# The first 65 microseconds of a two-block kernel: load order, a constant tile for TensorE, and when the first modulation is turned

## The chip, the cores and the metric

The kernel runs on one core of one Trainium2 chip. The metric is the device time of one execution in microseconds (us), as the median of several runs. All data are float32. The five engines run their own instruction streams and meet at semaphores: TensorE (PE, with its weight loads shown as PEld), VectorE (DVE), ScalarE (ACT), GpSimd (POOL) and SyncE (SP), which here issues all the DMAs. A float32 matmul of the program appears in the trace as two records.

## The reference, cut to what matters

The program computes a first block (an mLSTM mixer beside a Hyena mixer, then a mixture of 16 experts) and then two layers of a second block. Only the start of the first block is touched by the change:

```python
mod = (c @ w_ada[l] + b_ada[l])[:, None, :]
sh1, sc1, gt1, sh2, sc2, gt2 = jnp.split(mod, 6, axis=-1)
h = rms_norm(x, g_mix[l]) * (1 + sc1) + sh1
p = h @ w_in[l] + b_in[l]                       # w_in is 1024 x 3600
q, k, v, o, gates, hx = jnp.split(p, split_pts, axis=-1)
filt = hyena_filters(seq_len, ...)              # see below
y_h = hyena_mixer(hx, conv_hy_w[l], conv_hy_b[l], filt, hy_bias[l], hyena_norm_g[l])

def hyena_filters(L, w1, b1, w2, b2, w3, freq, deltas):
    hid = jnp.sin(fr * (z @ w1 + b1))           # z: 256 x 33 constant features
    hid = jnp.sin(fr * (hid @ w2 + b2))         # 256 x 64
    h = hid @ w3                                # 256 x 2048
    window = jnp.exp(-t * jnp.abs(deltas)) + HYENA_WINDOW_SHIFT
    return (h * window).reshape(L, HYENA_ORDER, HYENA_DIRS, HYENA_WIDTH)
```

x is 256 tokens by 1024 features. The filters are needed as spectra (two orders, each a real and an imaginary part, from a DFT written as matmuls), and the Hyena mixer splits hx into x1, x2 and z.

## The kernel before

Every engine's order is written out by hand; there is no scheduler. What goes before what on an engine is the order of the calls.

**Weights** come as a stream of 2 MB tiles (`stream`) into a ring of four such slots. SP issues them in order, and issues tile n when the slot that it needs is released by the matmuls that read it (`release`, `release_with`). The stream before starts ada0 to ada4, z, x1, q, ada5, x2, ... An "ada" tile is a quarter of the rows of a third of w_ada; four of them (ada0 to ada3) make the first 2048 columns of the modulation, in which the shift sh1 and the scale sc1 of h lie. A z, x1, q, ... tile is 512 columns of w_in.

**Modulation.** `ada()` takes the next step on each engine. On TensorE it multiplies one tile (`ada_rows`, L1255, 16 records). All of a third's tiles are summed in PSUM bank 7, the only bank for this. After the third's last tile ACT copies the row out of the bank. The step after that first multiplies the next tile (which waits for bank 7 to be free) and then turns the row into columns (`ada_turn`, L1272), which DVE adds to its bias (`turned`, L1800). From them DVE makes the scale A1 (L1869), and DVE (L1872) and ACT (last four row tiles) make h, which the projections wait for (`h_ready`, `ht_scaled`).

**Filters.** Two small matmuls, hid1 (L1287, 33 rows) and hid2 (L1291, 64 rows), each followed by some DVE arithmetic and a sine on ACT; then eight matmuls with 64 rows and 512 columns (L1299). ACT makes the decay windows from `dlt` (the decay rates `hy_deltas`, broadcast to all partitions) and a column of `minus_t`, which lies in the table `tab`. DVE multiplies windows and filters (L1841) and adds and subtracts the halves (L1843, L1844). `spectrum(o)` (L1310, eight records) is the DFT of order o; ACT and DVE bring it out of PSUM.

**Norm.** GpSimd squares x, TensorE sums the squares with a matrix of ones (`sums`, L1281), ACT and DVE make 1/rms (L1848) and DVE scales x with it (L1850).

**TensorE's order before** is hid1, hid2, ada0, filters, sums, ada1, spectrum(0), ada2, ada3, ada4 and turn, spectrum(1), project z, project x1. After that follow gates, q and the rest of the block (L1236 is the line of all those projections). The instances of `ada` behind this stretch keep their places in the change.

**SP's order before** is the small filter inputs, the parameters, ada0, the tables, `dlt`, x, ada1 to ada3, four small inputs (b_v, b_gates, w_gates, w_router), then the stream.

## Time and profile before

| | before |
|---|---|
| time, median of 3 runs | 2253.46 us (2251.59 to 2253.8) |
| span of the profiled execution | 2255.7 us |
| TensorE busy | 2007.8 us, 89% |
| VectorE, ScalarE, GpSimd busy | 582.6, 417.7, 194.1 us |
| DMA | 664.24 MB, mean 294 GB/s |

The profiled execution took 2.2 us more than the median. The table of 40 slices (56.4 us each) shows how the limits change: in the first slice TensorE has 7 tenths while the DMA engines are nearly full; in slices 2 and 3 TensorE is full and the DMA engines are half idle; from slice 6 to slice 25 (some 282 to 1410 us) the DMA engines are full at about 420 GB/s, which is the expert part; after that it is TensorE that is full.

### The profile page before, as it was taken

The page shows a single profiled execution, that of the slowest core. Times are in us where ns is not written, and L with a number is a line of the kernel's source. Part 1 is how long each engine was busy: PE and PEld are TensorE (multiplying, and loading weights), DVE is VectorE, ACT ScalarE, POOL GpSimd, SP SyncE. Part 2 cuts the span into 40 slices and gives each one's busy share as a digit, 9 for nine tenths or more (in the row PEclk, how much of TensorE's full clock was granted, in tenths as well). Part 3 has the DMA queues.
Part 4 walks back from the last instruction along what each step waited for, and adds up shares of the span by engine and source line. Part 5 has one row for each costly group of instructions (what it writes and reads, how often), then busy time and mean ns, then how long its engine had stood idle before and what let it go on. Part 6 is the DMA issues. An engine that isn't in the chain of part 4 may idle for free.

```text
span 2255.7 us, 32640 instructions
## 1 busy us (share of the span) xinstructions
PE 2007.8 (89%) x14140; PEld 1405.5 (62%) x14140; DVE 582.6 (26%) x1187; ACT 417.7 (19%) x766; POOL 194.1 (9%) x183
## 2 busy tenths in 40 slices
PE   7999889887888888987888877999999999999997
PEld 3866666542445545653565543756888877588886
DVE  5267220104421100000001201454432034630001
ACT  2122121202310100000000311435200033630001
POOL 0530000002000000000000000135000003600000
PEclk9999989898899999998999999999999999999999
DMA  9548899999999999999999999530487842144450
GB/s 364 207 171 332 325 421 424 400 426 425 409 388 426 426 426 420 421 417 423 420 419 426 426 379 414 141 135 23 165 298 226 192 148 82 34 148 151 126 154 19
DMA packets 181286, 664.24 MB, mean 294 GB/s; under 512 B 17335, under 2 KB 121304, under 8 KB 142552
## 3 DMA queue, kind: packets, MB, share of 16 engines
q1 hardware_dynamic: 181144, 662.15, 75.2%
q8 instruction: 112, 1.84, 0.3%
q14 instruction: 30, 0.25, 0.0%
HBM read 661.08 MB, written 1.05 MB: 294 GB/s over the span
## 4 chain that ended last, share of the span: by engine, by line
PE 47%; DMA 21%; ACT 4%; DVE 3%; issue 1%; POOL 0%; SPq 0%; ACTq 0%; DVEq 0%; POOLq 0%
PE ps L1148 19%; PE ps L650 9%; DMA ring<-in_context_weights 7%; DMA ring<-in_w_gate 6%; DMA ring<-in_w_down_slots 5%; PE ps L1531 4%; DMA ring<-in_w_up 3%; PE ps L1557 2%; PE ps L984 2%; PE ps L1157 2%; PE ps L951 2%; ACT arena L2434 1%; PE ps L846 1%; PE ps L676 1%; PE ps L1060 1%
## 5 line engine op out<-in xcount | busy, mean ns | idle before, releaser
L1148 PE MATMUL ps<-arena,ring 128*128 128x256 f32 x1984 | 429.9, 379 | 1.0 <-DVEq L389 0.9
L1148 PEld LDWEIGHTS ps<-arena,ring 128*128 128x128 f32 x1984 | 376.5, 190 | 54.2 <-issue 1.7
L1531 PE MATMUL ps<-ring,arena 128*32 128x256 f32 x4032 | 259.7, 404 | 87.7 <-DMA ring<-in_w_up 45.2
L650 PE MATMUL ps<-arena,ring 128*128 128x256 f32 (+2 forms) x1372 | 310.5, 386 | 6.7 <-DMA ring<-in_context_weights 6.6
L650 PEld LDWEIGHTS ps<-arena,ring 128*128 128x128 f32 (+2 forms) x1372 | 249.7, 188 | 73.8 <-DMA ring<-in_context_weights 24.3
L1531 PEld LDWEIGHTS ps<-ring,arena 128*32 128x32 f32 x4032 | 126.1, 114 | 205.3 <-DMA ring<-in_w_up 59.1
L2141 ACT ACTIVATE arena<-ps 128x512 f32<-128x512 f32 (+3 forms) x143 | 76.7, 536 | 740.3 <-PE ps L650 332.2
L1557 PE MATMUL ps<-ring,arena 128*32 128x512 f32 x1024 | 141.4, 682 | 58.8 <-DMA ring<-in_w_down_slots 51.9
L1557 PEld LDWEIGHTS ps<-ring,arena 128*32 128x32 f32 x1024 | 30.5, 119 | 155.9 <-DMA ring<-in_w_down_slots 85.2
L1236 PE MATMUL ps<-arena,ring 128*128 128x256 f32 x512 | 112.0, 380 | 1.4 <-DMA ring<-in_w_out 1.4
L2946 POOL TENSOR_TENSOR XC<-XC,arena 128x256 f32<-128x256 f32 x32 | 23.4, 730 | 992.5 <-ACT XC L2235 972.2
L1236 PEld LDWEIGHTS ps<-arena,ring 128*128 128x128 f32 x512 | 96.9, 190 | 18.1 <-issue 5.2
L2956 POOL TENSOR_SCALAR arena<-arena 128x512 f32<-128x512 f32 x48 | 78.7, 1639 | 82.4 <-DVE arena L2851 79.1
L650 PE MATMUL ps<-ring,arena 128*128 128x256 f32 (+3 forms) x312 | 85.7, 426 | 0.0
L951 PE MATMUL ps<-arena,ring 128*128 128x256 f32 x352 | 78.6, 381 | 3.9 <-DMA ring<-in_context_weights 3.9
L2605 DVE SCALAR_TENSOR_TENSOR XC<-ps,arena,XC 128x256 f32<-128x256 f32 x48 | 23.2, 484 | 225.8 <-PE ps L1148 144.3
L1773 ACT ACTIVATE arena<-ps 128x256 f32<-128x256 f32 x32 | 12.3, 384 | 357.7 <-PE ps L1531 357.6
L951 PEld LDWEIGHTS ps<-arena,ring 128*128 128x128 f32 x352 | 66.2, 190 | 18.5 <-DMA ring<-in_context_weights 8.3
L650 PEld LDWEIGHTS ps<-ring,arena 128*128 128x128 f32 x312 | 54.5, 190 | 26.9 <-issue 17.1
L2110 DVE TENSOR_TENSOR arena<-arena,ps 128x256 f32<-128x256 f32 x32 | 13.5, 421 | 214.9 <-ACT arena L1773 213.9
L2900 DVE TENSOR_TENSOR arena<-arena,ps 128x512 f32<-128x512 f32 x20 | 13.8, 688 | 212.3 <-PE ps L1148 212.3
L1255 PE MATMUL ps<-ring,arena 128*32 128x512 f32 x448 | 56.9, 636 | 10.7 <-DMA ring<-in_w_ada 9.0
(359 smaller groups left out, 1940.9 us busy)
## 6 DMA issues: line engine op xcount, KB each, us to landing
ring<-in_w_up SPq DMA_DIRECT2D x64, 2048.0 KB, 13.2
ring<-in_w_down_slots SPq DMA_DIRECT2D x64, 2048.0 KB, 14.4
ring<-in_w_gate SPq DMA_DIRECT2D x62, 2048.0 KB, 14.0
ring<-in_w_ada SPq DMA_DIRECT2D x36, 2048.0 KB, 9.8
ring<-in_w_ffn_in SPq DMA_DIRECT2D x44, 1024.0 KB, 7.7
ring<-in_context_weights SPq DMA_DIRECT2D x35, 1024.0 KB, 14.5
ring<-in_w_ffn_out SPq DMA_DIRECT2D x16, 1408.0 KB, 7.0
ring<-in_w_in SPq DMA_DIRECT2D x9, 2048.0 KB, 8.0
```

Source lines behind the costliest of these rows:

```text
L650: m = mm(o, a, x, start=(k == 0 and r == 0), stop=(k == kt - 1 and last))
L951: m = mm(b[i][:, T * x:T * x + T], w[:, k % 2, c:c + P], HID[:, k, :], start=(k == 0 and x == 0), stop=(k == 21 and x == 1))
L984: m = mm(b[:, 0:RAW], w[:, k, c:c + P], raw[:, k, :], start=(k == 0), stop=(k == KD - 1))
L1148: m = mm(b, w[:, k, c:c + P], src[:, k, :], start=(k == 0), stop=(k == kt - 1))
L1157: m = mm(b[:, 0:T], held["w"][:, k, c:c + P], oT[X][:, k, :], start=(k == 0), stop=(k == KD - 1))
L1236: m = mm(b[:, T * i:T * i + T], w[:, k, P * (j + i):P * (j + i) + P], src(k), start=(k == 0), stop=(k == ktiles - 1))
L1255: m = mm(row_bank[0][32 * g:32 * g + 32, :], cpad[:, 2 * h + k, :], w[:, k, W * g:W * g + W], start=(h == 0 and k == 0), stop=(h == 3 and ...
L1531: m = mm(b[u][32 * c:32 * c + 32, T * x:T * x + T], xs[:, 2 * h + k, CAP * e:CAP * e + CAP], w[:, k, at_:at_ + T], start=(h == 0 and k == ...
L1557: m = mm(b[a][64 * n + 32 * j:64 * n + 32 * j + 32, :], hdT[:, 2 * a + j, ch, :], w[:, j, at_:at_ + W], start=(i == 0 and odd == 0), stop= ...
L2141: step(a(dst, src, f, **kw), frees=name if frees else None)
L2946: step(nc.gpsimd.tensor_tensor(hat[st][n % 2][:, x, :], ex[st][n % 2][:, x, :], glqk[:, x, :], ALU.mult), lev_ready if x else None)
L2956: step(nc.gpsimd.tensor_scalar(Pr[n % 8], Pr[n % 8], sm[:, n % 8:n % 8 + 1], None, ALU.mult), pn_ready[X])
```

## The change

1. **Loads.** `dlt` and x go ahead of ada0, and the tables behind it. `minus_t` moves from the tables into the parameters, so that the windows need only `dlt` and the parameters. `dlt` has a semaphore of its own; GpSimd's convolutions wait for the parameters in place of the tables.
2. **Stream.** z takes the place of ada4 in the stream, and ada4 comes behind z. SP issues z ahead of the four small inputs.
3. **Constant tile.** DVE sets a tile of 640 columns to 1.0 as its first instruction. TensorE multiplies it one time ahead of hid1, two times behind it and four times behind hid2 (128x128 by 512 columns, into bank 7, never read).
4. **TensorE's order.** The filters are cut in two halves of four matmuls, with ada0 between them.
5. **The first turn** comes as a step of its own right behind ada3. h follows at once on DVE and ACT. ada4 and spectrum(1) come behind project z, and DVE's and ACT's work on spectrum(0) comes behind h.
6. A semaphore that nothing waited for (`gqa_normed_ctx`) is gone.

The core of the diff (the wait for `c_ready` of the first ada tile becomes 2, because the constant tile uses its first count):

```diff
-                    if i and i % 4 == 0:
+                    if i == 4:
+                        turn(tiles[3][0], 0)
+                        continue
+                    i -= i > 4
...
+                    if i > 4 and i % 4 == 0:
                         turn(tiles[i - 1][0], tiles[i - 1][1] // 4)
...
+            def warming(count):
+
+                for _ in range(count):
+                    mm(ps[ADA_BANKS[0]][:], warm[:, 0:P], warm[:, P:P + W], start=True, stop=True)
+
+            pe.wait_ge(c_ready, 1)
+            warming(1)
             pe.wait_ge(s_hid, 48)
...
+            step(v.memset(warm, 1.0), c_ready)
...
-            spectrum(0)
             ada(5)
             step(stt(out=A1, in0=mod[:, 8:16], scalar=1.0, in1=pc("g_mix", 0, 8), op0=ALU.add, op1=ALU.mult))
...
             tell(h_ready)
+            spectrum(0)
+            ada()
             spectrum(1)
```

TensorE's instructions from the start, before (L1255 is one ada tile for every 8, L1299 filters, L1281 sums, L1310 a spectrum, L1272 the turn, L1236 the projections):

```order
L1287 MATMUL ps<-arena 64x256
L1291 MATMUL ps<-arena 64x256
L1255 MATMUL ps<-ring,arena 32x512 x8
L1299 MATMUL ps<-arena 128x512 x8
L1281 MATMUL ps<-arena,tab 128x256 x8
L1255 MATMUL ps<-ring,arena 32x512 x8
L1310 MATMUL ps<-arena,tab 128x512 x4
L1255 MATMUL ps<-ring,arena 32x512 x24
L1272 MATMUL ps<-tab,arena 128x4 x4
L1310 MATMUL ps<-arena,tab 128x512 x4
L1236 MATMUL ps<-arena,ring 128x256 x64
```

The same stretch of the changed kernel, where L1294 is the constant tile, L1261 an ada tile, L1313 the filters, L1287 the sums, L1321 a spectrum, L1278 the turn and L1242 a projection:

```order
L1305 MATMUL ps<-arena 64x256
L1294 MATMUL ps<-arena 128x512 x4
L1313 MATMUL ps<-arena 128x512 x4
L1261 MATMUL ps<-ring,arena 32x512 x8
L1313 MATMUL ps<-arena 128x512 x4
L1287 MATMUL ps<-arena,tab 128x256 x8
L1261 MATMUL ps<-ring,arena 32x512 x8
L1321 MATMUL ps<-arena,tab 128x512 x4
L1261 MATMUL ps<-ring,arena 32x512 x16
L1278 MATMUL ps<-tab,arena 128x4 x4
L1242 MATMUL ps<-arena,ring 128x256 x32
L1261 MATMUL ps<-ring,arena 32x512 x8
```

One ada tile (ada4) and one spectrum, which stood beside the turn, now stand behind the first 32 matmuls of the projections (z).

SP's DMAs behind the parameters, before:

```order
L3001 DMA ring<-in_w_ada 128x2x2048
L3004 DMA tab<-in_tables 128x2878
L3005 DMA arena<-in_hy_deltas 128x2048
L3006 DMA XC<-in_xT 128x8x256
L3001 DMA ring<-in_w_ada 128x2x2048 x3
L3009 DMA arena<-in_b_v 128x512
```

And in the changed kernel:

```order
L3028 DMA arena<-in_hy_deltas 128x2048
L3029 DMA XC<-in_xT 128x8x256
L3026 DMA ring<-in_w_ada 128x2x2048
L3031 DMA tab<-in_tables 128x2876
L3026 DMA ring<-in_w_ada 128x2x2048 x3
L3026 DMA ring<-in_w_in 128x8x512
L3034 DMA arena<-in_b_v 128x512
```

The 2 MB of ada0 went from ahead of three loads to between them, and z (the w_in tile) to ahead of the small inputs.

## Rows read from the trace of the kernel before

**Rows 1.** The page: the span in 40 slices of 56.4 us.

```profile
PE   7999889887888888987888877999999999999997
...
DMA  9548899999999999999999999530487842144450
```

**Rows 2.** Timeline of PE, 0 to 60 us: start, us, engine, line, operation, count [idle before].

```profile
...
8.53 1.08 PE L1291 MATMUL ps<-arena 64*64 64x256 f32 x2 [3.91 <-ACT arena L1604]
14.14 3.64 PE L1255 MATMUL ps<-ring,arena 128*32 128x512 f32 x16 [4.53 <-DMA ring<-in_w_ada]
17.71 14.02 PE L1299 MATMUL ps<-arena 64*128 64x512 f32 x16
31.66 6.09 PE L1281 MATMUL ps<-arena,tab 128*128 128x256 f32 x16
...
43.16 3.64 PE L1255 MATMUL ps<-ring,arena 128*32 128x512 f32 x32
47.66 1.93 PE L1255 MATMUL ps<-ring,arena 128*32 128x512 f32 x16 [0.87 <-ACT arena L1604]
49.52 1.06 PE L1272 MATMUL ps<-tab,arena 128*128 128x4 f32 x8
50.44 3.68 PE L1310 MATMUL ps<-arena,tab 128*128 128x512 f32 x8
53.95 6.42 PE L1236 MATMUL ps<-arena,ring 128*128 128x256 f32 x29
```

**Rows 3.** DMA issues: KB, us from issue to landing (first row ada3 alone).

```profile
ring<-in_w_ada SPq DMA_DIRECT2D x1, 2048.0 KB, 20.5
...
tab<-in_tables SPq DMA_DIRECT2D x1, 1439.0 KB, 12.9
arena<-in_hy_deltas SPq DMA_DIRECT2D x1, 1024.0 KB, 15.0
XC<-in_xT SPq DMA_DIRECT2D x1, 1024.0 KB, 17.4
...
par<-in_params SPq DMA_DIRECT2D x1, 193.0 KB, 4.7
```

**Rows 4.** Timeline of SP, 0 to 60 us (the last row ends with ada3's issue).

```profile
3.43 0.59 SPq L2990 DMA_DIRECT2D par<-in_params  x1
...
4.56 0.46 SPq L3004 DMA_DIRECT2D tab<-in_tables  x1
5.06 0.43 SPq L3005 DMA_DIRECT2D arena<-in_hy_deltas  x1
5.54 0.43 SPq L3006 DMA_DIRECT2D XC<-in_xT  x1
...
17.38 0.57 SPq L3001 DMA_DIRECT2D ring<-in_w_ada  x1
```

**Rows 5.** Timeline of ACT and DVE around the filters and around h.

```profile
12.97 0.42 ACT L1604 ACTIVATE arena<-arena 64x256 f32<-64x256 f32 x1 [4.58 <-DVE arena L1829]
...
22.28 0.69 DVE L1841 SCALAR_TENSOR_TENSOR arena<-arena,ps 128x512 f32<-128x512 f32 x1 [9.41 <-ACT arena L1604]
...
36.80 0.69 DVE L1844 TENSOR_TENSOR arena<-arena 128x512 f32<-128x512 f32 x1
...
50.68 0.17 DVE L1800 TENSOR_TENSOR arena<-ps,par 128x16 f32<-128x16 f32 x1 [2.60 <-PE ps L1272]
...
51.15 2.50 ACT L1604 ACTIVATE arena<-arena 128x256 f32<-128x256 f32 x4 [3.63 <-DVEq L389]
```

**Rows 6.** Busy us and granted clock by stretch: stretch, length, PE (x) to POOL (x), PEclk.

```profile
227.00:230.00 3.00, 0.32 (x4) 0.00 (x0) 2.71 (x6) 0.00 (x0) 0.00 (x0) 1.00 0.99 388
...
231.00:234.40 3.40, 3.40 (x18) 0.59 (x16) 2.67 (x8) 0.00 (x0) 0.00 (x0) 0.51 1.05 388
```

**Rows 7.** The same view: TensorE behind the stretch that is changed.

```profile
68.00:210.00 142.00, 142.00 (x692) 99.71 (x691) 79.98 (x135) 32.05 (x50) 50.48 (x60) 1.00 0.57 213
```

**Rows 8.** Who waited for whom, SP's queue, 150 to 1410 us: total, times, longest.

```profile
SPq L3001 <- PE ps L1531: 565.9, 125, 20.2
```

More of the change, by code:

```diff
@@ L222, in build @@
         dlt = at(14376, 4 * W)
+        warm = at(4096, P + W)
         qkT = at(16424, 8, T)
@@ L395, in build @@
         s_load = sem("tables_loaded")
+        s_dlt = sem("decay_rates_loaded")
         s_hid = sem("filter_features_loaded")
@@ L439, in build @@
         six_ready = sem("six_tiles_summed")
+        gnorm_ready = sem("gqa_normed_x")
         ab_ready = sem("modulation_ready_ctx")
@@ L458, in ada_slot @@
             return w.rearrange("(k p) n -> p k n", p=P)[:, 2 * (j % 4):2 * (j % 4) + 2, 2048 * (j // 4):2048 * (j // 4) + 2048]
-        stream = [(f"ada{j}", ada_slot(w_ada, j)) for j in range(5)]
+        stream = [(f"ada{j}", ada_slot(w_ada, j)) for j in range(4)]
         column = {"q": 0, "k": 512, "v": 1024, "o": 1536, "x1": 2064, "x2": 2576, "z": 3088}
@@ L463, in build @@
         ada_tiles += [(f"ada{l}_{j}", ada_slot(I["w_ada_2"][l], j)) for l in range(2) for j in range((12, 4)[l])]
-        at_tile = 5
-        for n, count in (("z", 0), ("x1", 0), ("q", 1), ("x2", 1), ("v", 1), ("o", 1), ("k", 11)):
+        at_tile = 4
+        for n, count in (("z", 1), ("x1", 0), ("q", 1), ("x2", 1), ("v", 1), ("o", 1), ("k", 11)):
             stream += [(n, cols(w_in, column[n], 512))] + ada_tiles[at_tile:at_tile + count]
@@ L1245, in ada_rows @@
                 if j == 0 and name == "ada":
-                    pe.wait_ge(c_ready, 1)
+                    pe.wait_ge(c_ready, 2)
                 if j == 0 and name == "ada0_":
@@ L1287, in _ @@
             close_bank(mm(b[0:64, 0:T], hw1[0:33, :], hfe[0:33, :], start=True, stop=True), "hid1")
+            warming(2)
             pe.wait_ge(s_fil, 48)
@@ L1291, in _, with filters @@
             close_bank(mm(b[0:64, 0:T], hw2[0:64, :], hid[0:64, :], start=True, stop=True), "hid2")
-            ada()
-            pe.wait_ge(hid_ready, 2)
-            for o in range(2):
+            warming(4)
+            def filters(o):
                 for n in range(TT):
@@ L1300, in _ @@
                                        start=True, stop=True), f"filt{o}{n}{d}")
-            pe.wait_ge(s_load, 32)
-            sums("ss0", sq0, sq0_ready)
-            ada()
             def spectrum(o):
@@ L1310, in spectrum @@
                         close_bank(mm(b[:], dft["cs"[which]][:, n, :], KS(o, which, n), start=True, stop=True), f"{name}{o}{n}")
+            pe.wait_ge(hid_ready, 2)
+            filters(0)
+            ada()
+            filters(1)
+            pe.wait_ge(s_load, 16)
+            sums("ss0", sq0, sq0_ready)
+            ada()
             spectrum(0)
             ada(3)
-            spectrum(1)
             T1v = T1.rearrange("p (a b) -> p a b", b=T)
@@ L1378, in _ @@
             project("z")
+            ada()
+            spectrum(1)
             project("x1")
@@ L1624, in act_mixers @@
                 step(a((hid, hid2)[i][0:64, :], hid2[0:64, :], ACT.Sin), hid_ready)
-            act.wait_ge(s_load, 32)
+            act.wait_ge(s_fil, 48)
+            act.wait_ge(s_dlt, 16)
             for o in range(2):
@@ L1632, in act_mixers @@
                             act.wait_ge(win_used, k - 1)
-                        step(a(win[d], dlt[:, W * j:W * j + W], ACT.Exp, scale=tb("minus_t")[:, n:n + 1]), win_ready)
+                        step(a(win[d], dlt[:, W * j:W * j + W], ACT.Exp, scale=pc("minus_t", n)), win_ready)
+            act.wait_ge(s_load, 16)
             def root(name, out_, n, k):
@@ L1651, in act_mixers @@
             tell(ht_scaled)
-            even_samples("k", 1, KR[:, 2, :], KI[:, 2, :])
+            even_samples("k", 0, KR[:, 0, :], KI[:, 0, :])
+            ada()
             def qk_rows(part):
@@ L1680, in act_mixers @@
             hyena_rows(2)
+            even_samples("k", 1, KR[:, 2, :], KI[:, 2, :])
             hyena_rows(0)
@@ L1844, in dve_mixers @@
                     step(tt(KS(o, 1, n), hwt[:, 0, :], hwt[:, 1, :], ALU.subtract), ks_ready)
+            dve.wait_ge(s_load, 16)
             dve.wait_ge(s_x, 16)
@@ L1873, in dve_mixers @@
             tell(h_ready)
+            spectrum(0)
+            ada()
             spectrum(1)
@@ L2534, in head_normed @@
                     step(stt(out=x, in0=x, scalar=w, in1=src, op0=ALU.mult, op1=ALU.mult), frees=name)
-                    tell(gnorm_ready[st])
+                    if st == X:
+                        tell(gnorm_ready)
             def rotations(N):
@@ L3001, in load @@
                     sp.dma_start(v, src).then_inc(landed[n % LANES], 16)
+            sp.dma_start(dlt, I["hy_deltas"].to_broadcast([P, 4 * W])).then_inc(s_dlt, 16)
+            sp.dma_start(xT, I["xT"].rearrange("(k p) t -> p k t", p=P)).then_inc(s_x, 16)
             load(0)
             sp.dma_start(tab[:], I["tables1"]).then_inc(s_load, 16)
-            sp.dma_start(dlt, I["hy_deltas"].to_broadcast([P, 4 * W])).then_inc(s_load, 16)
-            sp.dma_start(xT, I["xT"].rearrange("(k p) t -> p k t", p=P)).then_inc(s_x, 16)
-            for n in range(1, 4):
+            for n in range(1, 5):
                 load(n)
@@ L3012, in _ @@
             sp.dma_start(wr, I["w_router"].rearrange("p (k n) -> p k n", k=KD)).then_inc(s_row, 16)
-            for n in range(4, n_before):
+            for n in range(5, n_before):
                 load(n)
@@ L3062, in kernel_arrays @@
     a["w_gates"] = by_tile(np.asarray(i["w_in"])[0][:, 4 * W:4 * W + NG])
-    one = {"c": i["c"], "b_qk": b_in[0:1024], "b_o": b_in[1536:2048], "b_hx": b_in[2064:3600]}
+    one = {"c": i["c"], "b_qk": b_in[0:1024], "b_o": b_in[1536:2048], "b_hx": b_in[2064:3600],
+           "minus_t": -by_parity(np.linspace(0, 1, T, dtype=np.float32))}
     parts = [c(one[n] if n in one else i[n]) for n, _ in COLS1]
```

17 lines of the change are left out of this document (7 added, 10 removed).

## The prediction

> **What bounds the kernel now.** Read the 40 slices first [rows 1]: the first slice has TensorE at 7 tenths with the DMA engines at 9, and the change touches only its first 68 us or so. So ask two questions: when does TensorE come to project x1, the first item behind the rearranged ones, and does a shift of that moment reach the end?
>
> The timeline of TensorE [rows 2] answers the first for the kernel before. It waits for DMA and for two sines until 14.14, and from there it has work without a gap of over 0.87 us, until the projections start behind spectrum(1) at 53.95. So from 14.14 the front is bound by TensorE, and at half speed for most of it: 16 records of an ada tile take 3.64 us at 14.14 and 1.93 us at 47.66; the 16 filter records take 14.02 us, 0.88 each, against 3.68 / 8 = 0.46 for spectrum records of the same 512 columns. The level changes from 1.2 to 2.4 GHz inside the sums: at the high level 16 records of 256 columns would take about 3.5 us (half of the 0.43 to 0.46 of 512 columns, each), and they took 6.09, so some 2 x (6.09 - 3.5) = 5 us of it ran low. What TensorE did before it rose: an ada tile, 14 us of 64-row matmuls, and then 5 us of matmuls with all 128 rows.
>
> A second reading of the same rows: the DMA engines were ahead of it. ada3 landed at 17.38 + 20.5 = 37.9 [rows 3, 4], and TensorE came to it at 43.16 + 1.8 = 44.9. **TensorE was 7.0 us behind its loads**, and those 7.0 us are all that a faster front can win there, since the bytes ahead of ada3 stay the same.
>
> For the second question: behind 68 us TensorE is busy for 142.00 of 142 us [rows 7], so a shift of x1 goes through unchanged up to 210 us. Behind that the DMA engines are nearly full [rows 1], but SP issues a tile when a slot is released, and its waits for such releases are long (565.9 us for one line of experts' matmuls alone) [rows 8], so its stream moves with TensorE's. I take the shift as passed on whole, in both directions.
>
> **The change part by part.**
>
> Loads. The parameters land at 3.43 + 4.7 = 8.1 as before. Then `dlt` takes 20.1 - 17.5 = 2.6 us and x 22.9 - 20.1 = 2.9 us, from the landings before at 17.5, 20.1 and 22.9 [rows 3, 4]. So `dlt` is there at 10.7 and x at 13.6. ada0 needs what it needed, 14.0 - 8.1 = 5.9 us, and comes at 19.5 in place of 14.0. The tables come at 23.0, and all four together end where they ended. ada1 to ada3 are not moved (37.9 for ada3). z follows at 42.9, since from x (22.9) to ada3 (37.9) three tiles took 5.0 us each; SP issues it when ada0 is released at about 21.5, with three tiles still queued, so the engines do not run dry. The small inputs come 5 us later than before, behind z, and nobody waits for them until the gates behind x1. ada4 lands near 49.5 and is needed at 59.
>
> Constant tile. Seven matmuls are 14 records, 0.85 to 0.88 us each at the low level. One matmul (1.7 us) fits ahead of hid1, which began at 8.53 - 3.91 - 1.1 = 3.5, two (3.4 us) into the 3.91 us wait ahead of hid2 [rows 2]. Four stand behind hid2, from 9.6 to 16.4 at the low level, while the second sine ends at 12.97 + 0.42 = 13.4 [rows 5]. They may delay the first filters by up to 3.0 us, but ada0 is not there before 19.6, so the cover is the wait for ada0: 19.6 - 16.4 = 3.2 us, enough for the first four filter matmuls only at the high level (8 x 0.44 = 3.5). DVE's extra fill of 640 columns ends well before hid1's result. These cost nothing by themselves.
>
> What they buy: they are 128-row matmuls for 6.8 us, and the sums raised the clock within 5 us. I take it as raised by 16.4, between the ends 13 and 16.4.
>
> TensorE up to ada3, at the high level: first filters until 17 to 20, ada0 19.6 to 21.5, second filters to 25.1, sums to 28.6 (the tables are there at 23.0, the squares of x before that), ada1 to 30.5, spectrum(0) to 34.1, ada2 to 36.0, then a wait for ada3, 38.0 to 39.9. DVE's filter chain took 36.80 + 0.69 - 22.28 = 15.2 us [rows 5]; it starts 7 us earlier and ends near 31; 1/rms and the eight products then end near 36. Both are covered. **Gain: 6.9 us** (ada3 begun at 38.0 in place of 44.9).
>
> The turn. Before, ada3 ends at 46.8, ACT's copy takes the 0.87 us gap, then ada4 and the turn (1.06), then spectrum(1) to 53.95. From the turn's end (50.58) to h's last part (51.15 + 2.50 = 53.65) are 3.07 us [rows 2, 5], and spectrum(1) covered them all. Now nothing does: ada3's end 39.9, + 0.87 copy, + 1.06 turn, + 3.07, + 0.15 start: z begins at 45.1. z takes 64 records of 6.42 / 29 = 0.22, so 14.0, ada4 1.9 and spectrum(1) 3.5, so x1 begins at 64.5. Before it began at 53.95 + 14.0 = 67.95. **This part costs 3.4 us** (idle time), and the sum so far is -3.5 us.
>
> The clock in that gap. From 39.9 to 45.1 TensorE has only eight 4-column records. The trace shows what follows such a gap: TensorE busy for 0.32 of the 3.00 us from 227 to 230, and from 231.0 to 234.4 a granted 0.51 [rows 6], which is 1.2 GHz. So I expect project z to start at, or fall to, the low level. Low time on full work costs half of itself. One such spell of 3.4 us costs at most 1.7; two of them in a row, with 1 us or more inside the gap, put up to 5.8 us of z at the low level, 2.9. From below: 1.2, if the spell begins in the gap. I take 2.1, nearer the middle of both. **Sum: -3.5 + 2.1 = -1.4 us.**
>
> A rule against the trace. The trace shows 17.6 us of back-to-back ada and filter matmuls at the low level before the clock rose in the sums [rows 2]: 64-row matmuls did not raise it. The Trainium skill's page "TensorE: Matmul & The Clock Gate", Part 1, says that the throttled state is the default and that sustained matmul activity releases it, without saying that rows count. By that rule the filters hold the clock once it is up; by the trace one cannot be sure. The sum above has the filters hold it; without that the third rival applies.
>
> Nothing else counts: the dropped semaphore was told but never awaited, GpSimd starts its convolutions with z, 9 us earlier, and had slack.
>
> **The rivals.** (a) The clock stays up through the gap: -3.5 us, 2250.0. For it: the turn's records may count as work. Against: rows 6. (b) An extra low spell takes in ada3: 2.0 us of waiting ahead of ada3 is already a gap, and a low ada3 costs 3.64 - 1.93 = 1.7 us, on the path, and up to 3.0 where ada2 or the sums are low too: -1.4 + 1.7 to -1.4 + 3.0, so 2253.8 to 2255.1. (c) The filters do not hold the clock: ada0 19.6 to 23.2, second filters 7.0 to 30.2, sums with 5 us low to 36.2, ada1, spectrum(0), ada2 and ada3 9.3 to 45.5, then 5.15 and z: x1 at 45.5 + 5.2 + 19.4 + 2.1 = 72.2, **+4.2 us**, 2257.7. It decides when ada3 is reached later than its landing, 38.0. (d) The change doesn't do what it says: the constant tile (all ones) raises nothing. Then the filters' first half ends at 23.4, ada0 at 27.0, the second half at 34.0, the sums begin 2.3 us later than before, and the uncovered 3.4 and the low spell of 2.1 come on top: +7.8, 2261.3.
>
> **How the numbers follow.** The forecast is no change that can be told: 2253.46 - 1.4 = 2252.1, the difference taken from the profiled execution (2255.7, 2.2 above the median) and put on the median. A measurement of this kernel can tell about 0.2%, 4.5 us. Chances: forecast 0.56, its own range 2250.3 to 2253.6; (a) 0.14, of which a third beyond -4.5 with smaller errors adding up; (b) 0.16; (c) 0.09, half of it beyond +4.5; (d) 0.05. Faster 0.05, slower 0.09, same 0.86. The range takes in (a) but for its low tail, (b) and the lower half of (c): 2249.2 to 2257.0.
>
> **What the profile of the changed kernel would show.** ada0's first matmul at 19.6; ada3's at 38.0 and with it the DMA engines as the front's bound; filter records of 0.43 us, not 0.85; TensorE idle for some 3.1 us ahead of project z, and z's 64 records taking 15 to 17 us in place of 14.0; x1 begun at 65 to 68. The forecast is wrong if x1 begins more than 4.5 us from 67.95, or if x1's shift and the span's differ by more than about 1.5 us, which would say that the front's shift is not passed on.

## The result: slower, by 5.3 us in the first measurement

| | before | after |
|---|---|---|
| median of 22 runs each | 2253.63 us (2249.67 to 2262.06) | 2258.89 us (2250.15 to 2270.59) |
| ratio, with its 95% interval | | 1.0024 (1.0014 to 1.0033) |
| span of the profiled execution | 2255.7 us | 2256.9 us |

The forecast was 2252.1 us with a range up to 2257.0. The changed kernel lies above it, and it scatters more: 20 us from lowest to highest, where before has 12.

The two profiled executions are not equally typical. In every whole kernel here the time of an execution is 1.7 to 1.8 us above its span. The span of 2255.7 us so stands for some 2257.5 us, 4 us above the median of before (the 2.2 us given ahead of the prediction sets a span against a time), while after's profiled execution took 2258.68 us, close to its median.

The profile after gives little of this away. First the page's 40 slices; they answer [rows 1]:

```profile
PE   8999889886788888986988877999999999999997
...
DMA  9548799999999999999999999531487842044450
```

The first slice went from 7 to 8 tenths: the constant tile is 11.6 us of matmuls, and the higher clock takes a good part of that off the others; the rest differs by a tenth here and there. The front is in TensorE's timeline (start, us, engine, line, operation, count, idle time before and who ended it). These rows answer [rows 2]:

```profile
9.61 5.71 PE L1294 MATMUL ps<-arena 128*128 128x512 f32 x8
15.24 3.70 PE L1313 MATMUL ps<-arena 64*128 64x512 f32 x8
19.35 1.92 PE L1261 MATMUL ps<-ring,arena 128*32 128x512 f32 x16 [0.41 <-DMA ring<-in_w_ada]
21.20 3.70 PE L1313 MATMUL ps<-arena 64*128 64x512 f32 x8
24.83 3.72 PE L1287 MATMUL ps<-arena,tab 128*128 128x256 f32 x16
...
38.33 1.92 PE L1261 MATMUL ps<-ring,arena 128*32 128x512 f32 x16 [2.44 <-DMA ring<-in_w_ada]
41.01 1.05 PE L1278 MATMUL ps<-tab,arena 128*128 128x4 f32 x8 [0.76 <-ACTq L389]
...
62.20 1.92 PE L1261 MATMUL ps<-ring,arena 128*32 128x512 f32 x16
64.06 3.70 PE L1321 MATMUL ps<-arena,tab 128*128 128x512 f32 x8
67.59 13.98 PE L1242 MATMUL ps<-arena,ring 128*128 128x256 f32 x64
```

Up to ada3 nearly all of it is as forecast: the clock is up by the first filters (8 records in 3.70 us, 0.46 each), ada0 begins at 19.35 (forecast 19.6), ada3 waits for its landing and begins at 38.33 (forecast 38.0). Then project z. The view by stretch (stretch, length, PE to POOL, granted clock, DMA share, GB/s) shows the turn's gap and what follows; it answers [rows 6, 7]:

```profile
40.25:45.25 5.00, 1.06 (x9) 0.97 (x8) 1.99 (x6) 3.00 (x5) 0.00 (x0) 0.92 1.08 399
45.30:51.20 5.90, 5.90 (x14) 4.74 (x15) 2.75 (x4) 1.16 (x2) 0.00 (x0) 0.50 1.01 396
...
68.00:210.00 142.00, 142.00 (x693) 99.73 (x693) 81.35 (x139) 31.07 (x48) 45.24 (x55) 1.00 0.57 217
```

z runs at 0.50 (1.2 GHz) until 51.2 and takes 16.9 us up to ada4. x1 begins at 67.59, against 67.95 before. So this execution has a front that is 0.4 us shorter and a span that is 1.2 us longer: either other executions have a longer front than this one, or something is lost behind it. Both turned out to be true.

### The profile page after: what moved, and what is told of

Read it like the earlier page. It is cut to its first block, busy times and chain, and to the rows that moved or that the text cites. A ratio compares the mean times of both kernels' runs of the same rounds, so it can differ in the third digit from the quotient of the medians.

```text
span 2256.9 us, 32668 instructions
## 1 busy us (share of the span) xinstructions
PE 2012.0 (89%) x14154; PEld 1406.7 (62%) x14154; DVE 579.5 (26%) x1188; ACT 417.4 (18%) x766; POOL 192.7 (9%) x183
## 3 DMA queue, kind: packets, MB, share of 16 engines
q8 instruction: 112, 1.84, 0.3%
## 4 chain that ended last, share of the span: by engine, by line
PE 47%; DMA 22%; DVE 4%; ACT 3%; issue 1%; POOL 0%; SPq 0%; ACTq 0%; DVEq 0%; POOLq 0%
PE ps L1154 19%; PE ps L656 10%; DMA ring<-in_context_weights 7%; DMA ring<-in_w_gate 6%; DMA ring<-in_w_down_slots 5%; PE ps L1550 4%; DMA ring<-in_w_up 3%; PE ps L1576 2%; PE ps L990 2%; PE ps L1163 2%; PE ps L957 2%; ACT arena L2458 1%; PE ps L852 1%; PE ps L1066 1%; PE ps L682 1%
## 5 line engine op out<-in xcount | busy, mean ns | idle before, releaser
L1242 PE MATMUL ps<-arena,ring 128*128 128x256 f32 x512 | 116.8, 391 | 6.0 <-ACTq L389 3.2
L1242 PEld LDWEIGHTS ps<-arena,ring 128*128 128x128 f32 x512 | 100.1, 197 | 23.2 <-issue 5.9
L1261 PE MATMUL ps<-ring,arena 128*32 128x512 f32 x448 | 56.2, 626 | 10.6 <-DMA ring<-in_w_ada 9.8
```

Of the source, the lines that this page charges most:

```text
L1242: m = mm(b[:, T * i:T * i + T], w[:, k, P * (j + i):P * (j + i) + P], src(k), start=(k == 0), stop=(k == ktiles - 1))
L1261: m = mm(row_bank[0][32 * g:32 * g + 32, :], cpad[:, 2 * h + k, :], w[:, k, W * g:W * g + W], start=(h == 0 and k == 0), stop=(h == 3 and ...
```

## The experiments

Every whole kernel was timed beside the kernel before on the same chip. A ratio and its interval are taken over the runs and need not be the quotient of the two medians. "Cut" kernels end behind project x1 and tell of the front alone (they leave out everything behind it, for before, after and the variants alike). Most executions of one of them lie within 1.5 us of each other, and so they show what the whole kernel's scatter hides. cut_before, cut_after and cut_hybrid ran on one chip; the other cut kernels ran on other chips, without a cut_before beside them, so differences of some tenths between those mean nothing.

### The front alone

Edit, the same in each kernel (the other engines stop at the same point, and x is sent out unchanged):

```diff
             project("x1")
+            raise Cut
```

> The kernel before, cut behind project x1: TensorE, ACT, DVE stop there, GpSimd only squares x, SP loads no tile behind q; x goes out unchanged. It is the front by itself, as the yardstick for the next one. The trace of before has x1's end at 67.95 + 14.0 = 82 us, so some 86 to 89 us in all. Both theories expect the same here: a spread of about 2 us from run to run, from where the clock rises in the sums.

> The changed kernel, cut at the same place in the same way. Theory F (the 5.3 us that the whole kernel lost are lost in the front, by low spells of TensorE's clock that the one profiled execution did not have): 4 to 6 us above cut_before in the median, with a spread of 5 us or more. Theory D (they are lost behind the front): at most 1 us from cut_before, as in the two profiles, where x1 began at 67.59 and 67.95.

Measured: before 89.48 us (88.85 to 89.71, 5 runs), after 89.98 us (89.31 to 94.24, 6 runs). Five of the six lie between 89.3 and 90.6, one at 94.24. So the usual front is 0.3 us (median of those five) to 0.5 us (of all six) longer, which is within the spread of either kernel, and not 4 to 6: Theory D. The one at 94.24 was the first sign of a second kind of front.

### ada4 and spectrum(1) back ahead of z

The hybrid keeps the loads, the constant tile and the early turn, and gives h's wait its old cover back (TensorE's part of the edit; the stream and the orders of ACT and DVE follow it):

```diff
             spectrum(0)
-            ada(3)
+            ada(4)
+            spectrum(1)
...
             project("z")
-            ada()
-            spectrum(1)
             project("x1")
```

> The whole changed kernel with one part undone: ada4 and spectrum(1) stand ahead of project z again (the stream has ada4 ahead of z again), and ACT and DVE bring spectrum(0) out ahead of h; loads, constant tile and the early turn stay. z begins near 49.5 (its landing), with no idle stretch of 5 us ahead of it, so x1 near 63.5. Theory F, with the loss in the uncovered wait for h: 4 us faster than before, 2249.5, and 9 below after. Theory D: 0 to 4 below before at the most, or, if what costs lies in any earlier arrival, above before as after is.

> The same with the cut behind x1. Theory F: 4 us below cut_before, 8 to 10 below cut_after. Theory D: 4 us below cut_before too, and 4 below cut_after.

Measured: the front 86.79 us (86.36 to 87.83), 2.7 under before and 3.2 under after; the whole 2252.45 against 2253.76 us, ratio 0.9993 (0.9984 to 1.0002). The forecast had charged 3.4 us for the uncovered wait and 2.1 us for the clock behind it, 5.5 in all. The hybrid wins back only 3.2 of this, because in cut_hybrid ada4 now waits 1.28 us for its own load, and ada4 and spectrum(1) run partly at the low level (3.01 and 4.26 us for 1.92 and 3.70). In the whole only 1.3 us of the front's 2.7 are seen; a stall of 1.40 us far behind the front, described below, is as much as the rest.

### What the gap costs in clock

Three constant matmuls (never read) in the gap, into bank 7, whose row ACT has copied out by then:

```diff
+            for _ in range(3):
+                mm(ps[ADA_BANKS[0]][:], ones, tb("idft_c"), start=True, stop=True)
             pe.wait_ge(h_ready, 1)
             pe.wait_ge(ht_scaled, 1)
             project("z")
```

> The kernel with the filled gap, cut off behind project x1 like the other cut kernels (all that follows is left out, x goes out unchanged). The changed kernel cut alike takes 89.98 us. Gap theory: 87.0 to 87.8, with z's 64 records in 14 to 14.5 us at a granted clock of 1.00. If the gap is not what lowers the clock: 89.5 to 90.5.

> The changed kernel with three constant matmuls (ones by a 512-column table, into bank 7, never read) right behind the first turn, where TensorE waits 3.2 us for h. If the low clock in project z comes from that gap, z takes 14.0 in place of 17.0 us and the whole is 2 to 3 us faster than the changed kernel. If the clock falls whatever stands in the gap: no difference. If the three matmuls outlast the wait for h (they take 2.6 us at the high level, 5.2 at the low one): up to 2 us slower.

Measured: the front 87.32 us (86.85 to 87.44), 2.7 under after. TensorE's timeline of cut_fill shows why, z in 14.05 us:

```profile
42.36 2.82 PE L1409 MATMUL ps<-tab 128*128 128x512 f32 x6
45.73 14.05 PE L1257 MATMUL ps<-arena,ring 128*128 128x256 f32 x64 [0.54 <-issue]
```

Against z's 16.98 us in after that is 2.9 (in the five profiles of the changed kernel z takes 15.97 to 16.98 us, so 1.9 to 2.9): the gap lowers the clock, and a filled gap does not. Yet the whole kernel gained nothing over before: 2257.07 against 2256.30 us, ratio 1.0000 (0.9990 to 1.0011), where the front is 2.2 us shorter than before's. The interval is too wide to show a loss behind the front by itself; fill's profile has a stall of 1.54 us there.

> The hybrid (loads, constant tile and early turn of the changed kernel, but ada4 and spectrum(1) ahead of project z) with the second half of spectrum(0) between ada2 and ada3 and done twice, so that TensorE does not stand idle ahead of ada3 (it waited 1 to 2.8 us there). If that wait is what lowers the clock in the turn, ada4 and spectrum(1): x1 begins near 63 in place of 65.3, and the time is 2 us under the hybrid's, 4 to 5 us under the kernel before. If the clock falls anyway: as the hybrid, 1 to 2 us under before.

> The same kernel cut off behind project x1 (all that follows is left out, x goes out unchanged). The hybrid cut alike takes 86.79 us. If the wait ahead of ada3 lowers the clock there: 84.3 to 85.3, with 1.9 us for ada4 and 3.7 for spectrum(1). If not: 86.3 to 87.3.

This edit held TensorE busy ahead of ada3 too (`spectrum(0, (0,))`, `ada()`, `spectrum(0, (1,), 2)`, `ada(3)`, `spectrum(1)` in place of `spectrum(0)`, `ada(4)`, `spectrum(1)`). The cut kernel took 86.87 us (86.73 to 89.96, 6 runs), no better than the hybrid. Its profile has ada4 at the high level (1.92 us) but z waiting 1.58 us for its own load, so a load took over as the bound. The whole took 2257.73 against 2253.55 us, ratio 1.0008 (0.9998 to 1.0019): 1.8 us over before by the ratio, where the cut kernel is 2.6 under. Its profile, of the slowest of its 12 executions, has enough to account for these 4.4: the stall (1.68 us), and z begun at 54.60, where the cut kernel's profile has 51.17.

### Does a shift of the front reach the end?

> The kernel before with each of the four matmuls of spectrum(1) done four times into its bank (the result is the same): 12 matmuls more at 0.92 us each, so project z and all behind it begin 11.0 us later. If a shift of the front is passed on whole, as the prediction took it: 11 us slower, 9.5 to 12.5. If the stretch behind absorbs part of it: 5 to 9 us slower, by what the experts' loads gain in the meantime.

```diff
-            spectrum(1)
+            spectrum(1, times=4)
```

(`times` is a new argument: each matmul is done that many times into its bank.)

Measured: 2267.58 against 2253.55 us, ratio 1.0055 (1.0037 to 1.0072), so 8 to 16 us for 11.0. That fits a shift that is passed on whole, as the forecast took it, and leaves room for a quarter of it to be absorbed.

> The kernel before once more, word for word, for a second profile of it and as a measure of what no change looks like. Ratio 1.000 within 0.0008 (2 us). Theory S (executions of one kernel differ by low spells of TensorE's clock that fall now here, now there behind 220 us): against the first profile of before the landings of the weights drift apart by 1 to 5 us behind 220 us in steps of about 1.7, though nothing was changed. Theory K (the changed kernels, whose landings are 2 to 6 us earlier than before's within the experts and lose as much again in the second block, do so because of the change): this profile agrees with the first one of before to within 1 us all along.

Measured: 2254.01 against 2253.55 us, ratio 0.9998 (0.9987 to 1.0009). In its profile SP issues the same tile of context weights 3.7 us earlier than in the first profile of before (655.86 for 659.53), and TensorE comes to the same matmuls 4.8 us earlier (1360.80 for 1365.64), though the kernel is the same and the front ended only 1 us earlier: Theory S, as far as the drift goes. So what two single profiles differ by behind 220 us says nothing of the change by itself. Its front was a surprise as well (TensorE's timeline; compare [rows 2]):

```profile
14.09 3.62 PE L1255 MATMUL ps<-ring,arena 128*32 128x512 f32 x16 [4.49 <-DMA ring<-in_w_ada]
17.64 7.13 PE L1299 MATMUL ps<-arena 64*128 64x512 f32 x16
26.66 5.38 PE L1281 MATMUL ps<-arena,tab 128*128 128x256 f32 x16 [1.90 <-issue]
...
45.23 3.41 PE L1255 MATMUL ps<-ring,arena 128*32 128x512 f32 x16 [4.13 <-DMA ring<-in_w_ada]
...
53.00 18.29 PE L1236 MATMUL ps<-arena,ring 128*128 128x256 f32 x84
```

The 16 filter records take 7.13 us in place of 14.02: here the clock rose right behind ada0, at least 14 us earlier than in the first profile. And yet z begins only 0.95 us earlier (53.00 for 53.95): TensorE stands still for 1.90 us ahead of the sums, and ada4 waits 4.13 us for its landing and then runs mostly at the low level (3.41 us). Two other profiles agree: cut_before, with 14.02 us for its filters, begins z at 53.32, and before_seven (below), with 7.13, at 52.77. **In four profiles of this order the start of z moves by 1.2 us, whether the clock rises early or late.** The profile that the forecast was made from has the latest z of the four.

### The changed kernel again, and its second front

> The changed kernel once more, word for word, beside the kernel before on this chip. In the first measurement it was 5.3 us slower (3.1 to 7.4), while its front alone, cut off behind project x1, was only 0.5 us slower. Theory L (some 4 us are lost behind the front, in every execution): 5 us slower again, ratio 1.002. Theory N (only the front's loss is real, and the rest is what executions scatter over 2.2 ms): 0 to 2 us slower, ratio 1.0000 to 1.0009.

> The changed kernel a third time. What has been found adds up to 2.1 us in most executions (0.5 in the front, 1.6 by the stall at matmul 6301), 2.7 to 3 in the mean if one in six has a front that is 4.8 us longer; the two measurements gave 5.3 and 2.0. If these causes are all: 1 to 4 us over the kernel before, and the stall near 1888 us again. If there is another loss of some 3 us: 4.5 to 7 over.

> The changed kernel cut off behind project x1 (all that follows is left out, x goes out unchanged), a second time: the first gave 89.3 to 90.6 us in five executions and 94.2 in one. It tells how often the longer front comes. If it is one in six or rarer: at most one of the executions above 92. If the longer front is what makes the whole kernel's 5.3 us: two or more of them near 94, and the median above 90.

Measured: after_again 2258.25 against 2256.30 us, ratio 1.0010 (1.0000 to 1.0021); after_third 2260.50 against 2253.73 us, ratio 1.0030 (1.0014 to 1.0047); cut_after_again 89.67 us (89.25 to 90.09, 5 runs). So the loss is real: in two of three measurements the interval lies above 1 (from 1.0014 in both), in the third it begins at 1.0000. TensorE's timeline of after_third shows where a part of it is:

```profile
9.35 3.70 PE L1294 MATMUL ps<-arena 128*128 128x512 f32 x8
13.25 3.70 PE L1313 MATMUL ps<-arena 64*128 64x512 f32 x8 [0.20 <-ACT arena L1623]
20.23 3.64 PE L1261 MATMUL ps<-ring,arena 128*32 128x512 f32 x16 [3.28 <-DMA ring<-in_w_ada]
23.80 7.19 PE L1313 MATMUL ps<-arena 64*128 64x512 f32 x8
30.92 6.38 PE L1287 MATMUL ps<-arena,tab 128*128 128x256 f32 x16
...
42.71 3.64 PE L1261 MATMUL ps<-ring,arena 128*32 128x512 f32 x32
47.12 1.05 PE L1278 MATMUL ps<-tab,arena 128*128 128x4 f32 x8 [0.76 <-ACTq L389]
51.39 16.73 PE L1242 MATMUL ps<-arena,ring 128*128 128x256 f32 x64 [3.22 <-DVEq L389]
...
73.44 6.85 PE L1242 MATMUL ps<-arena,ring 128*128 128x256 f32 x31
```

The clock was up for the first filters (3.70), TensorE then waited 3.28 us for ada0, and ada0, the second filters and the sums ran at the low level (3.64, 7.19, 6.38 in place of 1.92, 3.70, 3.72). ada3 no longer waits for its landing, z begins 6.1 us later than in the first profile of after, and x1 at 73.44 in place of 67.59. In its outcome this is the prediction's rival (c), a front of 4.2 us more than before, here 5.5. Its condition was another, though: not filters that fail to hold the clock (7.13 us for 16 records in before_again, 3.70 for eight in after), but a wait that loses it.

Where does the wait come from? The 11 profiles of kernels that have the constant tile fall in two groups, by what the last four constant matmuls (eight records) took:

| profiles | constant tile, us | wait ahead of ada0 | ada0 | second filters |
|---|---|---|---|---|
| after, hybrid, fill, cut_after_again, cut_hybrid | 5.58 to 5.88 | 0.20 to 1.09 | 1.92 | 3.70 |
| after_again, cut_after, cut_fill, cut_hybrid_held | 3.70 | 1.84 to 2.47 | 3.20 to 3.59 | 3.70 to 4.07 |
| after_third, hybrid_held | 3.70 | 3.28, 2.49 | 3.64 | 7.19 |

Where the clock rises amid the constant tile, TensorE comes to ada0 just before its landing and keeps the clock. Where it is up before them (by 9.6 us), the first filters end 2 us earlier, the wait ahead of ada0 grows to 1.84 us or more, and ada0 runs at the low level for most or all of it. **So the constant tile can raise the clock too early.** No run forced the rise to one moment or the other; this is read from 11 profiles, none of which speaks against it. What decides between the last two rows is open. The wait's length alone does not: cut_fill waited 2.47 us and had the clock back behind ada0,

```profile
19.58 3.59 PE L1276 MATMUL ps<-ring,arena 128*32 128x512 f32 x16 [2.47 <-DMA ring<-in_w_ada]
23.10 3.70 PE L1328 MATMUL ps<-arena 64*128 64x512 f32 x8
```

and hybrid_held waited 2.49 us and had not:

```profile
19.23 3.64 PE L1261 MATMUL ps<-ring,arena 128*32 128x512 f32 x16 [2.49 <-DMA ring<-in_w_ada]
22.80 7.19 PE L1313 MATMUL ps<-arena 64*128 64x512 f32 x8
```

How often does the longer front come? In the cut changed kernel one execution in 11 has it by its time (94.24 us, with a mean granted clock of 0.856, where the others have 0.909 to 0.947). In the whole kernel only the profiles tell: after_third, one of three. (hybrid_held's profile has it too.) Both have a mean granted clock of 0.959 over the whole execution; the other ten profiles of whole kernels have 0.962 to 0.970. Of the 46 executions of the changed kernel in its three measurements, 13 have 0.960 or less, and of 109 of the kernel before 7 have. Those 13 took 2264.8 us in the mean, the other 33 2257.4. If the 13 were all such fronts, they would add 7.5 x 13 / 46 = 2.1 us to the mean; at one in 11 and 4.5 us each it would be 0.4. The count of 13 is an inference that the record does not secure: some 16 us more at half speed lower the mean over 2260 us by 0.0035, while executions of the changed kernel scatter from 0.954 to 0.968, 7 executions of before reach 0.960 too, and the 13 are 7.5 us slower where the front has some 6. Whatever lowers the clock elsewhere is in it as well.

### The constant tile

> The changed kernel without its seven constant matmuls, cut off behind project x1 (all that follows is left out). If the constant tile is what raises the clock early: ada0 and all filters at 0.87 us a record, the sums begin near 34 us in place of 24.8, and the cut kernel takes 95 to 98 us (the prediction's case d: 7.8 us over the kernel before, 97.3). If the clock would rise by ada0 and the filters alone: 90 us, as with them.

> The changed kernel without its seven constant matmuls, whole. Its front alone was 0.5 us slower than the changed kernel's in the median. Theory C (seven instructions more bring a stall of 1.6 us in the second block): no stall near 1885, and 1 to 2 us under the changed kernel, 0.5 to 2.5 over the kernel before. Theory O: the stall stays, and the time is that of the changed kernel, 2 to 5 us over before.

```diff
             pe.wait_ge(c_ready, 1)
-            warming(1)
             pe.wait_ge(s_hid, 48)
```

(and `warming(2)`, `warming(4)` alike.) Measured: the front 90.43 us (89.44 to 95.27, 7 runs, two of them at 95), 0.5 to 0.8 over after; the whole 2255.81 against 2254.21 us, ratio 1.0011 (0.9999 to 1.0022). TensorE's timeline of no_warm:

```profile
13.50 7.19 PE L1310 MATMUL ps<-arena 64*128 64x512 f32 x8 [3.84 <-ACT arena L1620]
20.62 3.62 PE L1261 MATMUL ps<-ring,arena 128*32 128x512 f32 x16
24.16 3.70 PE L1310 MATMUL ps<-arena 64*128 64x512 f32 x8
```

Here the clock rises without the constant tile, behind ada0, at 24.2. What the seven constant matmuls gain earlier is not needed in such an execution, since TensorE only waits the longer for ada0 and ada3. But two of the seven cut executions took 95.10 and 95.27 us, within the 95 to 98 expected if the tile is what raises the clock early. The profile of cut_no_warm is of the first of them:

```profile
13.55 7.19 PE L1325 MATMUL ps<-arena 64*128 64x512 f32 x8 [3.83 <-ACT arena L1636]
20.67 3.64 PE L1276 MATMUL ps<-ring,arena 128*32 128x512 f32 x16
24.24 7.19 PE L1325 MATMUL ps<-arena 64*128 64x512 f32 x8
31.36 5.95 PE L1302 MATMUL ps<-arena,tab 128*128 128x256 f32 x16
...
73.24 13.98 PE L1257 MATMUL ps<-arena,ring 128*128 128x256 f32 x64
```

The clock rises inside the sums, and x1 begins at 73.24. So both answers are true, in different executions: the tile guards against a late rise (two in seven without it) and brings the wait ahead of ada0. The mean of all cut executions is 91.6 us without it and 90.2 with it (7 and 11 runs). In this profile the granted clock reads 1.00 from 20.2 to 31.0 us, though every record takes twice its time, and so it does from 18 to 31 us in the first profile of before: a mean granted clock does not show a low level that lasts from the start.

> The hybrid (ada4 and spectrum(1) ahead of project z again, early turn and load order of the changed kernel kept) without the constant matmuls, whole. Theory C: no stall near 1885, and so 1.6 us better than the hybrid (1.3 us under before) if the front is not slower without the constant tile: 2 to 3 us under before. If the constant tile is what makes the front early (hid2 to sums at the high clock): 0 to 2 us over before.

> The same, cut off behind project x1 (all that follows is left out, x goes out unchanged). The hybrid cut alike took 86.8 us and the kernel before 89.5. If the constant tile is worth nothing here: 86.5 to 87.3. If the late rise of the clock that one look at the changed kernel without it showed (sums at the low level until 36 us) is the rule: 89 to 91.

Measured: the front 87.17 us (86.45 to 87.92, 5 runs), 2.3 under before; the whole 2253.19 against 2254.21 us, ratio 0.9993 (0.9982 to 1.0004). Like the hybrid it is no slower than before and cannot be told from it; no kernel here beats before beyond its interval. What hybrid_no_warm lacks is the stall of the next section, and its front is 0.4 us longer than the hybrid's; the times cannot tell the two apart.

### A stall 1.9 ms further on

Comparing when VectorE's instructions start in the different profiles, the changed kernels lose 1.6 to 1.9 us against before at about 1890 us, always at the same place. TensorE's timeline of after there:

```profile
1884.85 0.85 PE L752 MATMUL ps<-arena,tab 128*32 128x128 f32 x12
1885.63 1.13 PE L656 MATMUL ps<-arena,ring 128*128 128x256 f32 x4
1888.39 3.94 PE L656 MATMUL ps<-arena,ring 128*128 128x256 f32 x17 [1.63 <-issue]
```

and of before:

```profile
1887.16 0.85 PE L746 MATMUL ps<-arena,tab 128*32 128x128 f32 x12
1887.94 7.17 PE L650 MATMUL ps<-arena,ring 128*128 128x256 f32 x32
```

"issue" means that TensorE stood still and waited for nothing that the profile shows, in the middle of a run of equal matmuls. Counted in TensorE's program, the stall is ahead of matmul 6301 (the first is 1) in each kernel; in the traces, which lack some records, 12334 matmul records stand ahead of it each time. fill has three matmuls more ahead of it, and its stall comes three matmuls earlier in the code. It is in all six profiles of whole kernels with the constant tile, 1.37 to 1.68 us each. Before has seven matmuls fewer up to there, so number 6301 falls nine matmuls into the run.

> The kernel before with seven tiny matmuls more (32x32 by 32 columns into bank 7, never read) in TensorE's wait ahead of hid2. They cost nothing there; they only make TensorE's program seven instructions longer, as the constant tile does. In all five profiles of changed kernels TensorE stands still for 1.4 to 1.7 us near 1883 to 1890 us with no waits shown, always at matmul 6301 of its program, and in two of the kernel before not. Theory C (the count does it): the profile shows such a stall of 1.4 to 1.7 us near 1885 to 1892 us, and the time is 1 to 2.5 us over the kernel before. Theory O (something else in the changed kernels does it): no stall, and the time within 1 us of before.

```diff
+            for _ in range(7):
+                mm(ps[ADA_BANKS[0]][0:32, 0:32], hw1[0:32, 0:32], hfe[0:32, 0:32], start=True, stop=True)
             pe.wait_ge(s_fil, 48)
```

Measured: 2256.82 against 2254.21 us, ratio 1.0006 (0.9996 to 1.0017), and in TensorE's timeline of before_seven the stall, two matmuls into the run as in after:

```profile
1883.15 1.13 PE L650 MATMUL ps<-arena,ring 128*128 128x256 f32 x4
1885.67 4.58 PE L650 MATMUL ps<-arena,ring 128*128 128x256 f32 x20 [1.38 <-issue]
```

no_warm and hybrid_no_warm, with the constant matmuls gone, have no such stall. Theory C holds: seven matmuls more, large or tiny, bring it. How long it is depends on more than the count: before_delay, with twelve more, has 0.45 us. (The times alone would not settle it: 1.4 us by the ratio, -0.9 to 3.8.)

What TensorE waits for is most likely its own program. The DMA view counts a queue for instructions; of after from 1885 to 1886 us (queue, packets, MB, share of 16 engines):

```profile
q1 hardware_dynamic: 160, 0.30, 80.8%
q8 instruction: 1, 0.02, 6.7%
```

The packet lies at 1885.8, and TensorE goes on at 1888.39, 2.6 us later. In before_seven and fill the same two are 2.4 and 2.5 us apart, in before_delay (where a stall of 0.45 us stands at the same matmul 6301) 2.3. In before the packet lies at 1888.1, and matmul 6301 is not due until 1887.94 + 9 x 0.45 = 1892.0, so it has 1.4 us to spare. In after other such packets lie at 1875.6, 1889.5 and 1896.3. That this one is TensorE's, and that the restart follows from it, is argued from these times and not shown. Why the packet comes no earlier was not tried; a load of weights fills the DMA engines until just then in these profiles.

The page of after counts such packets over the whole execution:

```profile
q8 instruction: 112, 1.84, 0.3%
```

The Trainium skill's page "Trainium Architecture — The Big Picture", The software stack, has the instruction streams moved into each engine when the program is loaded. Taken by itself, that would leave nothing to wait for later. This trace does not agree: 112 packets of some 16 KB (1.84 MB in all) come during the execution.

## Why the prediction was wrong, step by step

Three steps failed. The gain of 6.9 us was taken from one late execution of before; the front is 0.3 to 0.5 us longer, not 1.4 shorter. The wait ahead of ada0 was counted as cover, at no cost to the clock; in some executions it costs a front of 4.5 to 6 us more. And "nothing else counts" left out a stall of 1.4 to 1.7 us that the seven added matmuls bring. What of the 4.9 us between the means these do not cover stays open (see the sum below).

**Loads, constant tile, TensorE up to ada3.** The times are right in the profile of after: ada0 19.35 for 19.6, ada3 38.33 for 38.0, filter records 0.46 for 0.43. The clock's rise was put between 13 and 16.4. In five of 11 profiles it lies amid the eight constant records (5.71 us in place of 7.0 in after), by about 14; in the other six it is up by 9.6. With the rise at its early end the forecast itself had the first filters done at 17 and ada0 at 19.6, a wait of 2.6 us. It called the 2.0 us ahead of ada3 "already a gap" in rival (b) and put no price on this one. Measured: 1.84 to 3.28 us of wait in six profiles, and 3.20 to 3.64 us for ada0 in place of 1.92.

**Gain of 6.9 us.** This failed. The rows were read rightly (ada3 begun at 44.9 with its load there since 37.9 [rows 2 to 4]), but they came of one execution in which the clock rose at the sums. In before_again ada3 begins at 37.46 + 1.82 = 39.3, so after gains 1.0 us there. "The filters at the low level bound the front" was taken as a property of the kernel; before_again shows it gone (7.13 in place of 14.02 us) and z's start hardly moved, since ada4's landing is the next limit. The forecast had x1 at 64.5 + 2.1 = 66.6; the four usual fronts of the changed kernel have 66.96 to 67.79. The three other profiles of before's order (cut_before, before_again, before_seven) begin z 0.6 to 1.2 us ahead of the 53.95 that the forecast subtracted from. The cut kernels measure the sum that counts: +0.3 to +0.5 us, for a forecast of -1.4 (with ends -3.5 and +4.2).

**The turn, 3.4 us.** Right: 5.0 us from ada3's end to z for 5.2, of which 3.22 are idle ahead of z. That the hybrid's front is also 3.2 us shorter is a coincidence, since its ada4 waits and runs low in turn.

**The clock in the gap, 2.1 us.** Right in the mechanism and near in size: z took 15.97 to 16.98 us in five profiles in place of 14.05, so 1.9 to 2.9, in the mean 2.5. Filling the gap won 2.7 us in the cut kernel.

**The rivals.** (a) is excluded in the profiles: z ran low in all five of the changed kernel. (c) names the outcome of the longer front, at +5.5 us instead of +4.2, and the point from which it decides (ada3 reached later than 38.0), but not its cause, the wait ahead of ada0. A chance of 0.09 for it as the answer of all executions may have been fair; it holds in one of 11 cut executions and one of three profiles of the whole, and its share in the whole is open. (d) was priced at +7.8. Without the constant tile the clock still rises behind ada0 in most executions (0.5 to 0.8 us over after in the median), and in two of seven it rises in the sums, 5.6 to 5.8 us over cut_before. The forecast treated each rival as one answer for all executions.

**"64-row matmuls did not raise it."** The forecast set this row against the Trainium skill's page "TensorE: Matmul & The Clock Gate", Part 1. The same part of that page says of the start that it varies from run to run for the same kernel. The traces here agree: the 16 filter records of before took 14.02 us in one profile and 7.13 in another. That sentence weighed against the forecast and was not used. The row itself is not contradicted: in every profile here the clock was up within 0.8 us of the filters' start, or they stayed low to their end (14.02 us for 16 records, 7.19 for eight in no_warm and after_third). What no row of before could carry was that its late rise is usual.

**A shift is passed on whole.** Not contradicted (11.0 us came out as 8 to 16). But "nothing else counts" was wrong: the seven matmuls cost 1.4 to 1.7 us at 1888 us, by their number. No step of the forecast looked there, and the row that could have warned, an "issue" wait, is not in the profile of before at that place.

**The sum.** Shown are 0.3 to 0.5 us (usual front) and 1.6 (stall), 2.1 us at most. The means of all runs differ by 4.9 us (2259.5 for 46 runs of the changed kernel, 2254.6 for 131 of before), with a scatter of these means of about 1 us. The longer front is shown to exist; it brings 0.4 us at one in 11 and 2.1 if all 13 executions of low mean clock are of its kind. So between 0.7 and 2.4 of the 4.9 us stay open. The medians of the three measurements, 5.3, 2.0 and 6.8 us, differ by more than this, which fits a part that falls in some executions only.

## What to carry to other kernels

A term read from one execution should be asked whether it would be there in the next: where an engine's clock rises at a moment that varies, price the front for an early and for a late rise, and prefer the order whose end is bound by a load in both. Removing cover has a cost that the median does not show: in four profiles before begins z within 1.2 us, in five the changed kernel begins it within 6.2. Raising the clock early is worth nothing if the next thing is a wait that loses it again; price every wait behind the rise, not only the last. Filling a wait with idle matmuls paid where the work behind is on the path (2.7 us in the gap before z) and did not where a load ends the next wait anyway (cut_hybrid_held), and every matmul added also moves the program's count, so look for new "issue" waits far behind the edit.

## What the runs showed of the hardware

- An otherwise identical TensorE program with seven tiny matmuls more stood still for 1.38 us at its matmul 6301, 1.9 ms behind the place of the change (before_seven). In four kernels an instruction packet of 0.02 MB lies 2.3 to 2.6 us ahead of the restart.
- Of the same kernel, the clock's first rise came right behind ada0 (at 17.6 us) in one profile and inside the sums (begun at 31.66 us [rows 2]) in another. The granted clock that the profile gives reads 1.00 in the low stretch ahead of that first rise (before, 18 to 31 us); only the records' durations show it.
- Waits of 0.20 to 1.09 us ahead of ada0 left the clock up (1.92 us for the tile, five profiles), waits of 1.84 to 3.28 us did not (3.20 to 3.64 us, six profiles). Behind two waits of nearly one length the clock came back with the tile in one kernel (2.47 us, then 3.70 for eight filter records) and did not in another (2.49 us, then 7.19).
